# Expert weights of a two-layer encoder: down rows taken four to a partition, gate and up columns taken with a step of four

## What is computed

```
def swiglu(h, w1, w3, w2):
    return (jax.nn.silu(h @ w1) * (h @ w3)) @ w2

logits = jnp.einsum('nd,de->ne', x, w_router)
top_logit, top_e = lax.top_k(logits, 2)
gates = jax.nn.softmax(top_logit, axis=-1)
# tokens are sorted by expert into blocks; for a block xi of expert e:
yb = swiglu(xi, w1[e], w3[e], w2[e])      # w1, w3: 1024 x 3584, w2: 3584 x 1024
y[token] += gate * yb
```

## Time and profile before

| | us |
|---|---|
| median of 3 runs (2776.61 to 2781.42) | 2779.08 |
| the profiled execution | 2778.44 |
| its span, from the first to the last instruction | 2776.7 |
| TensorE busy with matmuls in the span | 2515.4 (91%) |
| TensorE busy with weight loads | 2137.4 (77%) |
| VectorE busy | 613.5 (22%) |
| ScalarE busy | 478.4 (17%) |
| matmuls of L858, on both halves of the slots | 405.9 + 516.4 |

### The profile page before, as it was taken

One profiled execution on the slowest core, in us unless ns is written; L12 is line 12 of the kernel. 1 busy time (PEld: TensorE's weight loads), 2 busy tenths in 40 slices (PEclk: granted clock), 3 DMA queues, 4 the chain that ended last, 5 costly groups with the idle time before them and its releaser, 6 DMA issues.

```text
span 2776.7 us, 38202 instructions
## 1 busy us (share of the span) xinstructions
PE 2515.4 (91%) x16064; PEld 2137.4 (77%) x16065; DVE 613.5 (22%) x1325; ACT 478.4 (17%) x980; POOL 116.8 (4%) x101
## 2 busy tenths in 40 slices
PE   8999998999999999957969988989969889898993
PEld 5557546888876466537969988989969889898993
DVE  2235334334632353330000000000000000001002
ACT  1124322222321243211000001010100010100102
POOL 2020100000010110010000000000000000000001
PEclk9999999999999999978989999999989989999996
DMA  7200343232221010156865565767757657588672
GB/s 239 76 31 14 98 158 119 93 105 98 84 78 70 31 44 8 45 195 244 300 233 197 199 251 198 266 226 288 287 194 270 255 217 297 209 314 302 238 288 107
DMA packets 203429, 483.69 MB, mean 174 GB/s; under 512 B 4849, under 2 KB 31616, under 8 KB 202864
## 3 DMA queue, kind: packets, MB, share of 16 engines
q1 hardware_dynamic: 192208, 429.36, 42.2%
q0 software_dynamic: 8576, 41.87, 4.8%
q10 hardware_dynamic: 2448, 9.44, 0.8%
HBM read 460.98 MB, written 35.39 MB: 179 GB/s over the span
## 4 chain that ended last, share of the span: by engine, by line
PE 76%; issue 6%; DVE 1%; DMA 1%; POOL 0%; ACT 0%; POOLq 0%; DVEq 0%; ACTq 0%
PE ps L858 32%; PE ps L873 15%; PE ps L768 9%; PE ps L617 5%; PE ps L779 4%; PE ps L625 2%; PE ps L704 2%; PE ps L724 2%; PE ps L610 2%; PE ps L826 1%; PE ps L842 1%; DMA attention_arena<-rows_by_slot 0%; DVE x_rows L1489 0%; POOL rows_by_slot L565 0%; DMA attention_arena<-results_by_slot,gains 0%
## 5 line engine op out<-in xcount | busy, mean ns | idle before, releaser
L858 PE MATMUL ps<-hT,weight_ring 128*128 128x128 f32 (+4 forms) x3072 | 405.9, 291 | 132.1 <-issue 132.1
L858 PE MATMUL ps<-hT,attention_arena 128*128 128x128 f32 (+4 forms) x4096 | 516.4, 283 | 0.0
L858 PEld LDWEIGHTS ps<-hT,attention_arena 128*128 128x128 f32 x4096 | 501.6, 191 | 0.0
L858 PEld LDWEIGHTS ps<-hT,weight_ring 128*128 128x128 f32 x3072 | 394.0, 198 | 133.9 <-issue 133.9
L1478 DVE TENSOR_TENSOR attention_arena<-ps,attention_arena 128x256 f32<-128x256 f32 x224 | 95.2, 425 | 1349.1 <-ACT attention_arena L1110 1349.1
L1110 ACT ACTIVATE attention_arena<-ps 128x256 f32<-128x256 f32 x224 | 86.1, 384 | 1128.5 <-PE ps L858 1128.4
L873 PE MATMUL ps<-attention_arena 128*128 128x128 f32 (+4 forms) x2048 | 266.0, 283 | 0.0
L617 PE MATMUL ps<-weight_ring,hT 128*128 128x384 f32 (+3 forms) x768 | 258.8, 498 | 3.3 <-DVE hT L1136 1.7
L873 PEld LDWEIGHTS ps<-attention_arena 128*128 128x128 f32 x2048 | 254.1, 191 | 0.0
L617 PEld LDWEIGHTS ps<-weight_ring,hT 128*128 128x128 f32 x768 | 147.1, 193 | 106.6 <-issue 62.4
L768 PE MATMUL ps<-x_high,w_parts 128*128 128x512 f32 x704 | 223.0, 398 | 5.5 <-ACT x_high L1006 5.5
(11 more groups left out here) (171 smaller groups left out, 1636.2 us busy)
## 6 DMA issues: line engine op xcount, KB each, us to landing
attention_arena<-in_e_w_dram SPq DMA_DIRECT2D x96, 2048.0 KB, 12.3
weight_ring<-in_e_w_dram SPq DMA_DIRECT2D x72, 2048.0 KB, 12.3
weight_ring<-in_w_dram SPq DMA_DIRECT2D x22, 1024.0 KB, 7.1
weight_ring<-in_w_dram SPq DMA_DIRECT2D x4, 2816.0 KB, 9.8
attention_arena<-rows_by_slot POOLq DMA_DIRECT2D x9, 1024.0 KB, 12.8
results_by_slot<-attention_arena ACTq DMA_DIRECT2D x9, 1024.0 KB, 9.8
weight_ring<-in_w_o_dram SPq DMA_DIRECT2D x4, 2048.0 KB, 8.1
weight_ring<-in_w_in_dram SPq DMA_DIRECT2D x2, 3072.0 KB, 10.9
```

The source lines that it names most:

```text
L858: last = nc.tensor.matmul(ps[:, f % 2, m * UNIT:m * UNIT + n], w[:, k, i * P:(i + 1) * P], XT[:, k, 0:n], start=(k == 0), stop=(k == ND - 1))
```

## The change

Two lines change. The load of a down part reads the chunk's 512 rows as `(p f)` in place of `(f p)`: partition p now takes the four neighbouring rows 4p, 4p + 1, 4p + 2, 4p + 3. In HBM these are one run of 16 KB, where there were four runs of 4 KB. Step i of the chunk then sums over the rows 4p + i, and so its hidden values must be the columns 4p + i of gate and up: `w[:, k, i::FC]`, 128 columns with a step of four floats (16 bytes) in each partition. The down product still reads 128 neighbouring columns of its slot.

```
                 else:
-                    src = a["e_w2"][0][e][c * FC * P:(c + 1) * FC * P, :].rearrange("(f p) c -> p f c", p=P)
+                    src = a["e_w2"][0][e][c * FC * P:(c + 1) * FC * P, :].rearrange("(p f) c -> p f c", p=P)
                     sp.dma_start(down[p % SLOTS], src).then_inc(slot_in[p % SLOTS], 16)
...
                     for k in range(ND):
-                        last = nc.tensor.matmul(ps[:, f % 2, m * UNIT:m * UNIT + n], w[:, k, i * P:(i + 1) * P],
+                        last = nc.tensor.matmul(ps[:, f % 2, m * UNIT:m * UNIT + n], w[:, k, i::FC],
                                                 XT[:, k, 0:n], start=(k == 0), stop=(k == ND - 1))
```

## The result

The changed kernel took 3580.27 us (median of 3 runs, 3575.02 to 3580.50) against 2779.08: a ratio of 1.2879, with an interval of 1.2853 to 1.2904. That is 801 us slower. The forecast was slower at 3491, with a range from 2772 to 3560: the direction came, and so did the place of the loss, the loads of L858; the term for them was too small.

A forecast was written before the change was run, and what follows sets the result against it. TensorE was taken to bound the kernel, by its pace of pairs and the gaps between units. Profiled 2778.4 + 712.1 for the strided loads + 0.6 to the runs' median gave 3491 us, range 2772 to 3560.

The forecast's parts named there:

- What bounds the kernel: In the experts, TensorE's pace of pairs inside units and instruction gaps between them (132.1 us); weights arrive in time.
- The down load at nothing: Down parts arriving as 128 runs of 16 KB instead of 512 of 4 KB cost nothing; at most 3 us gained.
- The load without slack: At L858 a 128-column weight load lasts about as long as the pair: hidden, with 0 to 3 ns spare at 128 and 132.
- the price of the strided load: At L858, 7168 loads with a step of four floats: 219 ns a pair instead of 111.6, in total 712.1 us more.
- the lower of these: Of 215 and 236 ns for a strided load's columns, 215: twice as long per column, giving 219 ns a pair.
- The forecast's own range: For the strided load at L858: 3440 us (a pair of 212 ns) to 3560 us (229 ns).
- ends of 111.6 and 440 ns: Bounds for a pair at L858: load priced by number of columns (111.6), or by bytes passed over (440).
- the load counts columns only: Rival, loads at L858: the step costs nothing, 2779 us, or 2776 with the down load's gain; chance 0.20.
- Half the price: Rival at L858: only part of each extra line is paid, 164 ns a pair, 318 us more, 3097; chance 0.10.
- The clock: Rival in the experts: TensorE's clock stays low, 1286 us more, 4065; chance 0.08 together with the full-bytes price.
- Longer or shorter gaps: Rivals between units, load free: fetches wait behind long runs, 2786 to 2815 (0.04), or fewer runs shorten gaps, 2767 (0.08).
- the faster rival: Between units: load free, fetches wait for the number of runs ahead, fewer runs shrink gaps up to 23 us, 2767; chance 0.08.

The follow-up runs named there:

- the step of two: Kernel before, but down parts in runs of 8 KB and gate and up loads taking every second column (8 bytes): 2805.46 us, ratio 1.0090.
- the step of eight: Kernel before, but gate and up loads taking every eighth column (32 bytes), down parts as before: 3615.36 us in one run.

## Why the prediction was wrong in size

**What bounds the kernel** held: no wait for weights came or went, and the loss lies in the pace of the pairs. **The down load at nothing** held, shown by the run that has it alone. **The load without slack** held, shown by the run with the step alone, which has the whole loss, and by the changed kernel, where 128 and 176 columns have one pace.

**The step that failed is the price of the strided load.** Between 215 and 236 ns for 128 columns I took "the lower of these" and had 219 ns a pair; it is 233.1. The one that I took, twice as long per column, does not ask how long the step is, and the step of two, 117.8 ns, refutes it. The other is nearer: 236 for the columns, and 111.6 + 236 - 107.7 = 240 for the pair, 3% too much. But its reason does not hold either. It let the load pay for the bytes that it passes over, and the step of eight passes over twice as many for 238 to 240 ns. What the load pays for is the pieces of 16 bytes that it enters; these grow as the bytes do up to a step of 16, and so the two sums meet at the step of this change. That the transposes' 59 ns are close to the 58 ns of 32 pieces may be more than chance, but no run tests it.

So it is partly luck that 3491 came within 3% of the result: neither of the two reasons was the right one. The forecast's own range ended at 229 ns a pair, and so at 3560, 20 us short of the result. With ends of 111.6 and 440 ns and no row of a strided load, 212 to 229 was too narrow.

The sum can be closed. 7168 x 0.2331 = 1670.9 us, 813.2 more than the 857.7 of before. Of the rest, most is a term that I had left out of the sum: after each gap the clock is low, and pairs with neighbouring columns are slower there (64 took 9.59 us in place of 7.1), while strided ones are not. The chain of the changed kernel between two units of 128 columns:

```profile
2126.11 13.74 issue
2139.85 15.19 PE ps L858 x64
```

15.19 us where 64 x 233.1 ns are 14.92. Over the eight units such rows sum to 20.0 us over the pace before and 3.6 after, 16.4 less. The first pair of the experts starts 4.0 us later than in the earlier trace rows, 2.3 of it by the longer wait for the rows:

```profile
1272.33 4.10 PE L858 MATMUL ps<-hT,weight_ring 128*128 128x132 f32 x16 [4.15 <-issue]
```

The seven gaps behind it, 131.2 - 4.15 against 132.1 - 4.72, are 0.3 us shorter: 813.2 - 16.4 + 4.0 - 0.3 = 800.5, against 801.9 between the two spans.

The chances on the rivals: *the load counts columns only* (0.20) is refuted by the change itself. The formula of the Trainium skill that went with it (TensorE: Matmul & The Clock Gate, section LDWEIGHTS: the number of columns divided by 1.2, in ns, with no term for a step between them) would give 107 ns; neighbouring columns agree with it here, 110 ns a pair in the earlier trace rows, and strided ones do not, 233.1 ns. *Half the price*, 164 ns a pair, is refuted by the same 233.1. *The clock* stayed at 0.96 in the stretch, where the earlier trace rows have 0.95, and the down step at 1.79 us. *Longer or shorter gaps* by the runs: neither. But the reason behind the faster rival, that weights in flight lengthen the gaps, is right as far as it goes: with the traffic away the gaps fell by 45 us. What was wrong there is that the number of runs matters: with a quarter of them in a down part the gaps were 130.0 us.

The rule on lines of 16 bytes (the Trainium skill, Advanced Engine Details and Errata, section SBUF Cachelines) pointed the right way. Its sentence "Need at least two hits on a cacheline to absorb SRAM access latency" fits to 6 ns: a step of 8 bytes, two columns per piece, costs 117.8 ns in place of 111.6. By the runs the price is 1.8 ns for each piece entered, a slope between 8 and 16 bytes.

## What to carry to other kernels

A layout that makes a transfer neater is paid for where the data are read: before a stationary operand gets a step, compare the pair's pace with 1.8 ns times the pieces of 16 bytes that its columns enter (as measured here, for 128 columns of float32), and look first whether the transfer was waited for at all. Where two values for an unknown price come from different mechanisms, and no row tells which of them is at work, taking the lower has no ground; the range should hold both. A short run with another step tells them apart: by the columns, by the bytes passed over, or by the pieces entered.

## What I had not expected of the hardware

A strided load does not follow the granted clock. Windows of L858, first the changed kernel, then the one before, each with a stretch at the lower clock and one at the full one (us, PE and PEld busy with instructions in brackets, PEclk, DMA share, GB/s; the counts include those at the edges):

```profile
2140.00:2145.00 5.00, 5.00 (x22) 5.00 (x23) 0.50 0.17 61
2157.00:2164.00 7.00, 7.00 (x32) 7.00 (x31) 1.00 0.00 0
```
```profile
2405.00:2408.50 3.50, 3.50 (x18) 3.50 (x18) 0.50 0.41 149
2434.00:2437.00 3.00, 3.00 (x29) 3.00 (x29) 1.00 1.00 309
```

Strided, 4.4 pairs per us at a granted clock of 0.50 (1.2 GHz) and 4.6 at 1.00 (2.4 GHz): the same pace but for the edges. With neighbouring columns, 5.1 and 9.7. So what limits the strided load does not go with the clock that TensorE is granted.

And a gap between units comes mostly with the jump to another copy of the body: with one copy it is about 4 us, and one instruction packet moves in it; with 16 copies it is 13 to 25 us, with three packets or more. The first unit, which takes that way too, has 4.7 us and one packet; why is open.
